# Attention scores of three mixers: from full-precision products on half the TensorE rows to float32r products on all 128 rows, with query and key split

## What is computed

```python
s_own = jnp.einsum('bhqd,bhkd->bhqk', qc, k_own).astype(jnp.float32) * scale + b_own        # moba
s = jnp.einsum('bhcqd,bhckd->bhcqk', qb, k).astype(jnp.float32) * scale                      # diff
s = jnp.einsum('bhrnqd,bhrnkd->bhrnqk', qb, kband).astype(jnp.float32) * scale               # dil
p = jax.nn.softmax(s, axis=-1)
```

## Time and profile before

| what | value |
|---|---|
| median of three runs (lowest, highest) | 3069.56 us (3068.42, 3072.04) |
| span of the profiled execution, first to last instruction | 3071.7 us |
| TensorE busy | 3000.4 us, 98% |
| VectorE busy | 1356.1 us, 44% |
| ScalarE busy | 795.1 us, 26% |
| GpSimd busy | 1657.0 us, 54% |
| mean granted TensorE clock | 0.994 of full speed |
| moba, first score to end of mixer | about 51 to 135 us |
| diff | about 161 to 245 us |
| dil | about 718 to 800 us |

### The profile page before, as it was taken

How to read it: one execution, slowest core, us unless ns; L and a number is a source line. 1 busy time by engine, 2 the same in 40 slices (tenths; PEclk the granted TensorE clock), 3 DMA queues, 4 the chain that set the end, 5 groups by cost and what they waited for, 6 DMA issues and landing times.

```text
span 3071.7 us, 44245 instructions
## 1 busy us (share of the span) xinstructions
PE 3000.4 (98%) x14668; PEld 2368.5 (77%) x14668; DVE 1356.1 (44%) x2331; ACT 795.1 (26%) x1455; POOL 1657.0 (54%) x1254
## 2 busy tenths in 40 slices
PE   8998999999999999999999999999999999999998
PEld 6766888886678888777688878888767788778886
DVE  3254544223445442244434476640543344576622
ACT  3343222112432220154421132210263411222201
POOL 4334666664156666533356646676424366556674
PEclk9998999999999999999999999999999999999999
DMA  6252233322122233212322222332213222222232
GB/s 159 78 165 82 95 97 100 109 93 86 32 69 96 96 106 103 97 42 76 83 74 101 86 76 96 96 106 101 69 39 98 64 97 92 82 82 96 96 113 79
DMA packets 99747, 276.64 MB, mean 90 GB/s; under 512 B 38014, under 2 KB 38782, under 8 KB 99634
## 3 DMA queue, kind: packets, MB, share of 16 engines
q1 hardware_dynamic: 97184, 269.03, 27.6%
q10 hardware_dynamic: 2450, 6.13, 0.9%
HBM read 271.39 MB, written 11.54 MB: 92 GB/s over the span
## 4 chain that ended last, share of the span: by engine, by line
PE 72%; DVE 2%; issue 1%; ACT 1%; DVEq 0%; ACTq 0%
PE PA L485 11%; PE PA L487 11%; PE PA L486 11%; PE PB L485 9%; PE PB L487 9%; PE PB L486 9%; PE O L726 2%; PE S L680 2%; PE T L591 2%; DVE hl L1484 1%; DVE tmps L1523 1%; PE O L517 1%; PE PB L743 0%; PE O L524 0%; ACT probs L1245 0%
## 5 line engine op out<-in xcount | busy, mean ns | idle before, releaser
L467 POOL TENSOR_TENSOR wl<-raw,wh 128x1024 fp32r<-128x1024 f32 (+2 forms) x416 | 1125.4, 2705 | 33.4
L464 POOL TENSOR_TENSOR zero<-zero 128x1 f32<-128x1 f32 x416 | 82.5, 198 | 1350.1 <-PE PA L487 611.2
L485 PE MATMUL PA<-hh,wh 128*128 128x512 f32 x1328 | 536.8, 404 | 12.8 <-DVE hl L1484 12.8
L487 PE MATMUL PA<-hh,wl 128*128 128x512 f32 x1328 | 519.2, 391 | 0.0
L486 PE MATMUL PA<-hl,wh 128*128 128x512 f32 x1328 | 519.0, 391 | 0.0
L465 POOL CAST wh<-raw 128x1024 fp32r<-128x1024 f32 (+2 forms) x416 | 475.1, 1142 | 0.0
L485 PE MATMUL PB<-hh,wh 128*128 128x512 f32 x896 | 357.2, 399 | 1.2 <-DVE tmps L1869 1.2
L487 PE MATMUL PB<-hh,wl 128*128 128x512 f32 x896 | 349.4, 390 | 0.0
L486 PE MATMUL PB<-hl,wh 128*128 128x512 f32 x896 | 349.1, 390 | 0.0
L485 PEld LDWEIGHTS PA<-hh,wh 128*128 128x128 f32 x1328 | 250.2, 188 | 117.8 <-issue 45.2
L487 PEld LDWEIGHTS PA<-hh,wl 128*128 128x128 f32 x1328 | 250.2, 188 | 53.3
(11 more groups left out here) (331 smaller groups left out, 4767.0 us busy)
## 6 DMA issues: line engine op xcount, KB each, us to landing
raw<-in_w_up SPq DMA_DIRECT2D x176, 512.0 KB, 3.4
raw<-in_w_down SPq DMA_DIRECT2D x64, 768.0 KB, 4.3
raw<-in_w_merge SPq DMA_DIRECT2D x48, 768.0 KB, 4.3
raw<-in_w_out SPq DMA_DIRECT2D x32, 512.0 KB, 3.4
strips_na<-in_rpb SPq DMA_DIRECT2D x1, 7620.0 KB, 32.1
raw<-in_w_pool SPq DMA_DIRECT2D x12, 512.0 KB, 3.4
raw<-in_w_na_qk SPq DMA_DIRECT2D x12, 512.0 KB, 3.5
raw<-in_w_na_v SPq DMA_DIRECT2D x8, 512.0 KB, 3.4
```

The lines of the kernel that those rows point to most:

```text
L464: nc.gpsimd.tensor_tensor(zero[:, :], zero[:, :], zero[:, :], ALU.add)
L467: nc.gpsimd.tensor_tensor(wl[s][:, 0:width], raw[s][:, 0:width], wh[s][:, 0:width].bitcast(F), ALU.subtract).then_inc(w_split, 1)
L485: mm(dst, h_, rh, start=first, stop=False)
L487: return mm(dst, l_, rh, start=False, stop=last)
```

## The change

In moba, diff and dil the scores become float32r products over all 128 rows. The scaled query tile stays in PSUM (`scale_query`), ScalarE writes its float32r rounding (`query_high`), VectorE writes what is left (`query_low`); for each head, high and low part are stacked on the 128 rows. The key is treated alike: ScalarE writes the high part twice, on both halves of the rows (`key_high`, four operations), VectorE writes the low part once (`key_low`) beside 64 rows of zeros. A score product is now two passes of 128 rows: stacked query x high key twice, then stacked query x low key and zeros. This leaves out low x low.

`pa_taken` and `pb_taken` are now set by `query_low` and `key_low`, which VectorE executes two steps (key of group 3: one step) after the scaling. ScalarE executes `query_high` and `key_high` in the step of the scaling, after `soften` and ahead of the copy of the transposed probabilities. The table `FILL` now covers 24 steps: parts lie denser in steps 0 to 10, and steps 11, 16, 21, 22 and 23 have none. `Y_TURN` moves one product with the denominators from step 15 to step 14. For buffers the change uses the last third of `wh` and `wl`, `acc`'s place, and three new tiles.

```diff
-FILL = {"moba": [3, 3, 2, 2, 3, 3, 0, 0], "axial": [3, 3, 2, 0, 0, 0, 0, 0]}
-FILL["diff"] = FILL["dil"] = FILL["na"] = FILL["moba"]
+SPLIT_KINDS = ("moba", "diff", "dil")
+FILL = {"na": [3, 3, 2, 2, 3, 3, 0, 0] * 3, "axial": [3, 3, 2, 0, 0, 0, 0, 0] * 3,
+        "moba": [3, 3, 3, 3, 4, 3, 3, 2, 3, 3, 2, 0, 2, 2, 2, 2, 0, 2, 2, 2, 2, 0, 0, 0]}
+FILL["diff"] = FILL["dil"] = FILL["moba"]
+Q_SCALE, Q_LOW = {3: 1, 8: 2, 16: 3, 29: 4}, {5: 1, 10: 2, 18: 3, 31: 4}
+K_SCALE, K_LOW = {5: 1, 11: 2, 21: 3, 35: 4}, {7: 1, 13: 2, 22: 3, 37: 4}
+TAKE_OF = {"moba": 0, "diff": 4, "dil": 8}
 Q_AT, K_AT = 3, 6
-Y_TURN = {"moba": (15, 23, 27, 35), "diff": (20, 28, 33, 41)}
-Y_TURN["axial"] = (15, 23, 27, 35)
-Y_TURN["dil"] = Y_TURN["na"] = Y_TURN["moba"]
+Y_TURN = {"moba": (14, 23, 27, 35), "diff": (20, 28, 33, 41)}
+Y_TURN["axial"] = Y_TURN["na"] = (15, 23, 27, 35)
+Y_TURN["dil"] = Y_TURN["moba"]
...
         V = sb("V", [P, QT, S], F, inner)
-        q_sb = sb("q_sb", [P, S], F, inner)
-        k_sb = sb("k_sb", [P, S], F, inner)
-        qr_sb = sb("qr_sb", [P, S], F, inner)
-        kr_sb = sb("kr_sb", [P, S], F, inner)
+        whole = ExitStack()
+        q_sb = sb("q_sb", [P, S], F, whole)
+        k_sb = sb("k_sb", [P, S], F, whole)
+        qr_sb = sb("qr_sb", [P, S], F, whole)
+        kr_sb = sb("kr_sb", [P, S], F, whole)
+        whole.close()
+        stacked = [sb(f"stacked{i}", [P, S], FR, inner) for i in range(4)]
...
-        acc = sb("acc", [P, S])
+        whole = ExitStack()
+        acc = sb("acc", [P, S], F, whole)
+        whole.close()
+        in_acc = sb("in_acc", [P, S], FR)
+        low = [sb(f"low{i}", [P, S], FR) for i in range(3)]
...
+        behind = [t[:, 2 * S:3 * S] for t in (wh[0], wh[1], wl[0], wl[1])]
+        q_stack = (stacked[0][:, :], stacked[1][:, :]), (behind[0], behind[1])
+        k_high_twice = (stacked[2][:, :], stacked[3][:, :]), (behind[2], in_acc[:, :])
+        k_low_once = (low[0][:, :], low[1][:, :]), (low[2][:, :], behind[3])
+        rows = slice(0, 64), slice(64, 128)
...
-                slots = FILL[kind] * 3 + list(last_plan)
+                slots = FILL[kind] + list(last_plan)
...
+                    if kind in SPLIT_KINDS:
+                        q = q_stack[g % 2][head][:, qt * P:qt * P + P]
+                        mm(SB[head][:, 0:span(t)], q, k_high_twice[g % 2][head][:, 0:span(t)], start=True, stop=False)
+                        mm(SB[head][:, 0:span(t)], q, k_low_once[g % 2][head][:, 0:span(t)], start=False,
+                           stop=True).then_inc(s_ready, 1)
+                        return
...
+            def query_high(n):
+                act.wait_ge(q_scaled, n + 1)
+                A(q_stack[n % 2][0][rows[0], :], PA[rows[0], :], ACT.Copy)
+                A(q_stack[n % 2][1][rows[1], :], PA[rows[1], :], ACT.Copy).then_inc(q_high, 1)
+            def key_high(n):
+                act.wait_ge(k_scaled, n + 1)
+                for head in range(2):
+                    A(k_high_twice[n % 2][head][rows[head], :], PB[rows[head], :], ACT.Copy)
+                A(k_high_twice[n % 2][0][rows[1], :], PB[rows[0], :], ACT.Copy)
+                A(k_high_twice[n % 2][1][rows[0], :], PB[rows[1], :], ACT.Copy).then_inc(k_high, 1)
...
+                    if kind in SPLIT_KINDS and t in Q_SCALE and (Q_SCALE[t] < 4 or kind == "moba"):
+                        query_high(TAKE_OF[kind] + Q_SCALE[t])
+                    if kind in SPLIT_KINDS and t in K_SCALE and (K_SCALE[t] < 4 or kind == "moba"):
+                        key_high(TAKE_OF[kind] + K_SCALE[t])
...
+            query_high(0); key_high(0)
...
+            query_high(TAKE_OF["dil"]); key_high(TAKE_OF["dil"])
...
+            def scale_query(b):
+                dve.wait_ge(entry_done, b["e"] + 3)
+                STT(out=PA[:, :], in0=PA[:, :], scalar=-0.125, in1=rs[:, :], op0=ALU.mult, op1=ALU.mult).then_inc(q_scaled, 1)
+            def scale_key(b):
+                dve.wait_ge(entry_done, b["e"] + 4)
+                TT(PB[:, :], PB[:, :], rs[:, :], ALU.mult).then_inc(k_scaled, 1)
+            def query_low(n):
+                dve.wait_ge(q_high, n + 1)
+                q = q_stack[n % 2]
+                TT(q[0][rows[1], :], PA[rows[0], :], q[0][rows[0], :].bitcast(F), ALU.subtract)
+                TT(q[1][rows[0], :], PA[rows[1], :], q[1][rows[1], :].bitcast(F), ALU.subtract).then_inc(pa_taken, 1)
+            def key_low(n):
+                dve.wait_ge(k_high, n + 1)
+                for head in range(2):
+                    r = rows[head]
+                    ins = TT(k_low_once[n % 2][head][r, :], PB[r, :], k_high_twice[n % 2][head][r, :].bitcast(F), ALU.subtract)
+                ins.then_inc(pb_taken, 1)
...
-                    elif t < 24 and t % 8 == Q_AT:
+                    elif kind == "na" and t < 24 and t % 8 == Q_AT:
                         take_q(ahead(g), g + 1)
-                    if kind != "axial" and t < 24 and t % 8 == K_AT:
+                    if kind == "na" and t < 24 and t % 8 == K_AT:
                         take_k(ahead(g), g + 1)
+                    if kind in SPLIT_KINDS:
+                        n = TAKE_OF[kind]
+                        of = lambda m: ahead(m - 1) if m < 4 else after
+                        if t in Q_LOW and (Q_LOW[t] < 4 or kind == "moba"):
+                            query_low(n + Q_LOW[t])
+                        if t in Q_SCALE and (Q_SCALE[t] < 4 or kind == "moba"):
+                            scale_query(of(Q_SCALE[t]))
+                        if t in K_LOW and (K_LOW[t] < 4 or kind == "moba"):
+                            key_low(n + K_LOW[t])
+                        if t in K_SCALE and (K_SCALE[t] < 4 or kind == "moba"):
+                            scale_key(of(K_SCALE[t]))
                     if gate is not None and t == 35:
                         take_gate(gate, 0)
-                    if after is not None and t == 29:
+                    if kind == "axial" and t == 29:
                         take_q(after, 0)
-                    if after is not None and t == 36:
+                    if kind == "axial" and t == 36:
                         take_k(after, 0)
...
-            take_q(H("moba_q0"), 0); take_k(H("moba_q0"), 0); v_copy(H("moba_v"))
+            scale_query(H("moba_q0")); scale_key(H("moba_q0")); query_low(0); key_low(0); v_copy(H("moba_v"))
...
-            take_q(H("dil_q0"), 0); take_k(H("dil_q0"), 0)
+            scale_query(H("dil_q0")); scale_key(H("dil_q0"))
+            v.memset(k_low_once[1][1][rows[0], :].bitcast(F), 0.0)
+            query_low(TAKE_OF["dil"]); key_low(TAKE_OF["dil"])
```

More of the change, by code:

```diff
@@ L323, in build @@
         rot_taken = sem("rot_taken")
+        q_scaled, q_high, k_scaled, k_high = (sem(n) for n in ("q_scaled", "q_high", "k_scaled", "k_high"))
         kr_rot, kr_done = sem("kr_rot"), sem("kr_done")
@@ L1950, in _ @@
             v.memset(eps[:, :], EPS).then_inc(dvc, 1)
+            for i in range(2):
+                v.memset(k_low_once[i][0][rows[1], :].bitcast(F), 0.0)
+                v.memset(k_low_once[i][1][rows[0], :].bitcast(F), 0.0)
             for k, s in enumerate(creds):
```

## The result

The changed kernel takes 3091.76 us (median of 4 runs, 3091.58 to 3093.18) against 3070.8 us for the one before (4 runs, 3068.42 to 3072.24). The ratio is 1.0069, with an interval of 1.0057 to 1.0081. The prediction was 3073.0, with a range up to 3080. It had too little loss in it, not the wrong sign of the sum: it said 3.5 us more, and there are 21. (Of all launches in this study one took 3762.12 us, of the kernel with the first group unsplit; the ratios leave it out.)

What follows compares the result with a forecast made beforehand. TensorE was taken to bound the kernel, with 72% of the chain. A gain of 14.0 us against costs of 17.5 us made 3.5 us more, so 3073.0 us, with a range of 3061.5 to 3080.

Steps and rivals of the forecast that it cites:

- The gain of 14 us: Score products in moba, diff and dil: cheaper passes save 1.22 us a group, 14.0 us in all.
- Cost 1: Start of dil: first scores wait for the query and key splitting, nothing covers it, +4.0 us.
- Cost 2: Start of moba: key subtraction delays the value copies and the second free score bank, +2.0 us.
- Cost 3: Step 21 of moba and dil: key copies delay the turned probabilities, TensorE idles 2.4 us, +2.0 us in each.
- Cost 4: Step 11 of moba and dil: the same wait with two parts between, +1.0 us in each.
- Cost 5: Step 29 in moba: query copies for diff with no part in steps 29 and 30, +1.3 us.
- Cost 6: Diff: splitting behind VectorE's softmax difference, +3.0 us at step 21, +1.4 at step 11, -0.2 in group 0.
- A copy at 0.54 us: ScalarE's splitting copies from PSUM: 0.54 us each with overlap, so query_high 1.1 us and key_high 2.2 us.
- The clock rival: Waits in diff and ahead of dil lower TensorE's granted clock: two more falls, 6.6 us, 3079.7 us; chance 0.2.
- Costed at nothing: Edits taken as off the path: earlier scaling, dil's memset, the 48 parts, GpSimd, the denominator product moved one step; 0 us.

Runs made afterwards that it cites:

- the schedule alone: Kernel before (float32 scores, no splitting) with the change's order of parts, take steps and denominators at step 14: 3065.89 us; on another chip 3070.16 us.
- the warm start of dil: Changed kernel plus eight float32 products that nothing reads, in TensorE's wait ahead of dil's first scores: 3088.31 us, ratio 1.0058 to the kernel before.

## Why the prediction was wrong

- **The gain of 14 us** was right by its prices (0.11, 0.12, 0.17 and 0.23 us a pass, no 0.20 around them; 256 columns are 0.12 apart, 215.50 to 215.62) and by its effect: 3.3 us shorter at the twelve undisturbed places of moba.
- **Cost 1, start of dil:** +4.0 predicted, +4.5 measured. **Cost 2, start of moba:** +2.0 and +2.1.
- **Cost 3, step 21:** idle 2.4 predicted, 2.43 measured. Step 20 to 24 was to take 8.9 us and took 10.5 (108.89 to 119.43). The 1.6 between them are the 1.7 of half clock, so without it the working stands.
- **Cost 4, step 11:** idle 1.0 predicted, 1.12 measured in moba (91.59) and 1.13 in dil (773.36).
- **Cost 5, step 29:** +1.3 predicted, +1.5 measured. TensorE waits 1.71 us at step 30 for turned probabilities that ScalarE copies at 134.52, behind the two query copies (133.31 and 133.90); in the kernel before it waits 0.21 for the same ones:

```profile
134.95 0.66 PE L750 MATMUL O<-probsT,V 128*64 128x128 f32 x8 [1.71 <-ACT probsT L1289]
```

```profile
128.24 0.66 PE L726 MATMUL O<-probsT,V 128*64 128x128 f32 x8 [0.21 <-ACT probsT L1251]
```

Behind it the clock is at 0.50 from 136.6 to 140.0, 1.7 us more. The two, less the 0.3 that the last pair of scores saves, are about the 3.0 us lost there.

- **Cost 6, diff:** at step 11 it was sized +1.4. Diff's group 1 went from 19.6 us to 23.4. The difference of the maps was costed at its usual time and took 2.56 us beside GpSimd's split, and the wait, reckoned at 2.3, became 3.57; 1.7 us of half clock follow it. Step 21 there came out as worked (8.7 predicted, 223.91 to 232.66 = 8.75 measured).
- **A copy at 0.54 us** was too little: starts are 0.60 apart, `key_high` is 2.4 and not 2.2. That is 0.2 at each place.
- **The step that failed is the clock.** The forecast had waits of 2.3 and 2.4 us in three mixers, and gave them no fall of the clock. The clock rival stood apart, with two falls for 6.6 us and a chance of 0.2, although its condition was only that a wait of such a size occurs, which the forecast itself contained. It was not a rival but a part of the forecast. By its own test (a stretch that showed 1.00 shows less) it held: moba's group 2 has 0.92 and diff's group 1 0.93. (Dil's first stretch didn't come under its 0.84, it shows 0.89, although the idle time ahead of it went from 3.61 to 8.10 us; there the clock was low before, too.) It measured 9.3 us. With it the sum would have been 3.5 + 9.3 = 12.8, 3082, still too little; the other 5.6 are, by rows of the ledger, diff (2.8), dil (1.8), the starts (0.6) and moba (0.4). In dil no single term was found for it.
- **Costed at nothing, and worth something:** the denominators at step 14 gain 1.1 us in moba and dil. I had looked only for what this product waits for, not for who waits for its bank.

What stays open: why the clock falls at a place in one execution and not in the next. The spread of the schedule alone, 3062.6 to 3074.4 us, goes with it: the granted clock of its executions under 3063 us is 0.995, of those over 3073 us 0.992, and 0.003 of 3070 us are 9. And one execution of each kernel stands behind the ledger, so that a difference of 1.7 us in a row can be one fall. Only at the start of dil was the clock's share shown by an edit; elsewhere it is read from the granted clock.

## What to carry over

When a change puts waits of about 2 us in front of a TensorE that is 98% busy, reckon each with a fall of the granted clock behind it at some of the places; here 2.4 us of idling cost 4.1. A cheaper product needs operands that somebody has to prepare: place that work in the other engine's order behind what the bound engine wants next, and look which bank it now holds longer. And run the schedule of a change without the change: here it was all that was gained.

## What the hardware showed that I had not expected

- A wait of 2.43 us was followed by 3.40 us at a granted clock of 0.50. The length of a wait alone does not tell whether that happens: at the start of moba TensorE waited 2.02 us in the changed kernel and ran at half clock behind it, and 2.05 us in the kernel with half of the key copies and did not. The end of moba fell behind a wait of only 1.71 us; in the kernel with the warm start of dil, whose moba is the same, the same wait is 1.70 and nothing falls (137 to 141 us at 1.00).
- Float32r passes on all 128 rows with a new weight tile each start 0.11 us apart at 128 columns and 0.12 at 256. Half the columns save nearly nothing there.
- A VectorE operation of 0.35 us took 2.56 us beside a GpSimd operation of 2.38 us that began 0.03 us after it. It did so at the same place of diff in all eight kernels that have both the new order and the split, and in no other.
- Copies of 64 x 512 out of PSUM cost ScalarE 0.59 us, as much as the 128 x 512 copy in the earlier trace rows: half the rows save nothing.
